# Sums of the up projections' weights: from VectorE to accumulating DMA transfers in DRAM

## The reference, cut to what matters

```python
h = x @ w_in + b_in                       # x: 1024 x 1024, w_in: 1024 x 5376
q_a, k_a, v_a, gate_a, q_b, k_b, v_b, gate_b, mg_a, mg_b = split(h)
o_a = swa_sink_attention(rope(q_a), rope(k_a), v_a, sinks) * silu(gate_a)   # 1024 x 512
y_a = o_a @ w_up_a                        # 512 -> 1024
o_b = stick_breaking_attention(q_b, k_b, v_b) * silu(gate_b)                # 1024 x 512
y_b = o_b @ w_up_b                        # 512 -> 1024
merged = sigmoid(mg_a) * y_a + sigmoid(mg_b) * y_b
out = layer_norm(alpha * x + merged @ w_out)
```

## Time and profile before

| what | value |
|---|---|
| median of 3 runs | 721.74 us (721.46 to 722.67) |
| the profiled execution | 722.17 us, span 720.4 us |
| PE busy | 707.2 us (98%) |
| DVE, ACT, POOL busy | 561.4, 446.7, 103.7 us |
| DMA moved | 77.27 MB, mean 107 GB/s |

### The profile page before, as it was taken

How to read it: one execution, slowest core, us unless ns; L and a number is a source line. 1 busy time by engine, 2 the same in 40 slices (tenths; PEclk the granted TensorE clock), 3 DMA queues, 4 the chain that set the end, 5 groups by cost and what they waited for, 6 DMA issues and landing times.

```text
span 720.4 us, 10882 instructions
## 1 busy us (share of the span) xinstructions
PE 707.2 (98%) x3998; PEld 577.8 (80%) x3998; DVE 561.4 (78%) x782; ACT 446.7 (62%) x776; POOL 103.7 (14%) x130
## 2 busy tenths in 40 slices
PE   8999999999999999999999999999998999999996
PEld 6888877777888888788888888888887888888885
DVE  6999788765987987898889784557779999990644
ACT  6954477776867767777686764565577655750421
POOL 0000000000322232132222310000000000000882
PEclk9999999999999999999999999999999999999999
DMA  8235332231100101020113214666324555830451
GB/s 297 113 90 126 107 94 84 74 98 43 50 31 30 60 30 59 3 88 16 45 30 117 74 45 144 219 233 208 117 82 153 170 166 159 310 118 1 160 190 58
DMA packets 44916, 77.27 MB, mean 107 GB/s; under 512 B 12352, under 2 KB 16960, under 8 KB 44864
## 3 DMA queue, kind: packets, MB, share of 16 engines
q1 hardware_dynamic: 44864, 76.59, 33.0%
HBM read 55.60 MB, written 18.87 MB: 103 GB/s over the span
## 4 chain that ended last, share of the span: by engine, by line
PE 96%; DVE 2%; DMA 1%; issue 1%; ACT 0%; SPq 0%; POOL 0%; POOLq 0%; DVEq 0%; ACTq 0%
PE ps L209 26%; PE ps L211 26%; PE ps L210 26%; PE ps L1789 5%; PE ps L1801 5%; PE ps L1774 4%; PE ps L1718 1%; PE ps L1730 1%; PE ps L1699 1%; DMA xr<-in_xt 1%; DVE keep L1455 1%; PE ps L1753 0%; PE ps L1687 0%; DVE o_t L1594 0%; DVE o_t L1585 0%
## 5 line engine op out<-in xcount | busy, mean ns | idle before, releaser
L209 PE MATMUL ps<-x_hi,w_hi 128*128 128x512 f32 x416 | 167.2, 402 | 1.9 <-DVE x_lo L1362 1.9
L211 PE MATMUL ps<-x_hi,w_lo 128*128 128x512 f32 x416 | 162.5, 391 | 0.0
L210 PE MATMUL ps<-x_lo,w_hi 128*128 128x512 f32 x416 | 162.2, 390 | 0.0
L1254 DVE TENSOR_TENSOR w_lo<-raw,w_hi 128x512 fp32r<-128x512 f32 x144 | 97.8, 694 | 47.9 <-ACT w_hi L772 47.4
L209 PE MATMUL ps<-t_ops,w_hi 128*128 128x512 f32 x288 | 115.8, 402 | 2.3 <-issue 2.3
L211 PE MATMUL ps<-t_ops,w_lo 128*128 128x512 f32 x288 | 113.2, 393 | 0.0
L210 PE MATMUL ps<-t_ops,w_hi 128*128 128x512 f32 x288 | 112.9, 392 | 0.0
L1455 DVE TENSOR_TENSOR_SCAN keep<-keep 128x895 f32<-128x895 f32 (+4 forms) x64 | 85.9, 1373 | 15.4 <-POOL keep L729 15.4
L209 PEld LDWEIGHTS ps<-x_hi,w_hi 128*128 128x128 f32 x416 | 78.2, 188 | 17.9 <-issue 3.4
L211 PEld LDWEIGHTS ps<-x_hi,w_lo 128*128 128x128 f32 x416 | 78.1, 188 | 16.8
L210 PEld LDWEIGHTS ps<-x_lo,w_hi 128*128 128x128 f32 x416 | 78.3, 188 | 14.6
(11 more groups left out here) (196 smaller groups left out, 1182.2 us busy)
## 6 DMA issues: line engine op xcount, KB each, us to landing
raw<-in_w SPq DMA_DIRECT2D x50, 256.0 KB, 2.9
raw<-in_w SPq DMA_DIRECT2D x24, 512.0 KB, 3.8
sig_m<-sig_d SPq DMA_DIRECT2D x16, 512.0 KB, 4.7
sig_d<-sig_m SPq DMA_DIRECT2D x28, 256.0 KB, 2.7
xr<-in_xt SPq DMA_DIRECT2D x16, 256.0 KB, 6.1
o_t<-o_d SPq DMA_DIRECT2D x8, 512.0 KB, 4.9
raw<-in_xn SPq DMA_DIRECT2D x8, 512.0 KB, 3.7
out<-o_t SPq DMA_DIRECT2D x16, 256.0 KB, 2.2
```

Source lines behind the costliest of these rows:

```text
L209: pe.matmul(out, w_hi, x_hi, start=first, stop=False, skip_group_check=goes_on)
L210: pe.matmul(out, w_hi, x_lo, start=False, stop=False, skip_group_check=goes_on)
L211: return pe.matmul(out, w_lo, x_hi, start=False, stop=last, skip_group_check=goes_on)
L1254: dve.tensor_tensor(ring_slot(w_lo, q), part_of(q), ring_slot(w_hi, q).bitcast(F32), ALU.subtract).then_inc(part_lo, 1)
```

## The change

For each of the four up pairs the seven weight operands are seven loads of 256 KB from DRAM, in the order of the products; DVE makes no weight sums for them. Three of the seven are quarters as they are. Four come from DRAM buffers (`up_sum_d`, 1 MB each, all four pairs in one) that POOL fills after the input has been split: three copies, then two accumulating transfers that wait for them, then a copy, an accumulating transfer and another one, each waiting for the one before. Two sums keep another sign than before; it is made good by the sign of two operands of the other side, by a scale of -1 when two products are read out, and by one subtraction. Five buffers take the loads in turn. The high parts of the weights go one to each product from product 138 on.

```diff
 def next_parts(q):
-    return {0: (q + 3, q + 4), 5: (), 6: (q + 3,)}.get(q % NP, (q + 4,)) if q < ALL_PRODUCTS - 4 else ()
+    if q >= LAST_PAIR + 5:
+        return (q + 4,) if q < ALL_PRODUCTS - 4 else ()
+    return {0: (q + 3, q + 4), 5: (), 6: (q + 3,)}.get(q % NP, (q + 4,))
+UP_RAWS = 5
+def up_raw_loads(q):
+    if q < LAST_PAIR + 3:
+        return {LAST_PAIR: (N_PRODUCTS, N_PRODUCTS + 1), LAST_PAIR + 1: (N_PRODUCTS + 2, N_PRODUCTS + 3),
+                LAST_PAIR + 2: (N_PRODUCTS + 4,)}.get(q, ())
+    return (q + 4 + UP_RAWS,) if q + 4 + UP_RAWS < ALL_PRODUCTS else ()
...
+        def up_raw(q):
+            n = (q - N_PRODUCTS) % UP_RAWS
+            return (raw[:, 1, half(0)], raw[:, 0, half(0)], w_x[:], raw[:, 0, half(1)], raw[:, 1, half(1)])[n]
+        up_tiles = w[UP_0:UP_0 + KT].rearrange("(j m) p c -> m p j c", m=2)
+        def up_quarter(m, kh):
+            return up_tiles[m][:, :, half(kh)]
...
+            def load_up(q):
+                n = q - N_PRODUCTS
+                if n < UP_RAWS:
+                    sp.wait_ge(part_lo, LAST_PAIR + (4, 5, 3, 6, 7)[n])
+                else:
+                    sp.wait_ge(part_lo, q - UP_RAWS + 1)
+                if n == 2:
+                    sp.wait_ge(w_sum, 4 * N_PAIRS)
+                    sp.wait_ge(up_summed, 16 * 8)
+                j, which = n // NP, ORDER[n % NP]
+                if which in up_sum_d:
+                    src = up_sum_d[which][:, j, :]
+                else:
+                    src = w[UP_0 + 2 * j + (which == 4)][:, half(which != 1)]
+                sp.dma_start(up_raw(q), src).then_inc(up_in[n % UP_RAWS], 16)
...
-                if pos < 2 and i + 1 < ALL_PAIRS:
+                if pos < 2 and i + 1 < N_PAIRS:
                     load_a1(i + 1, pos)
-                if pos == 2 and i + 1 < ALL_PAIRS:
+                if pos == 2 and i + 1 < N_PAIRS:
                     load_a2(i + 1)
+                for n in up_raw_loads(q):
+                    load_up(n)
...
+            pool.wait_ge(x_lo_done, 2 * KT)
+            pool.dma_start(up_sum_d[5], up_quarter(1, 0)).then_inc(up_summed, 16)
+            pool.dma_start(up_sum_d[7], up_quarter(0, 0)).then_inc(up_summed, 16)
+            pool.dma_start(up_sum_d[3], up_quarter(0, 1)).then_inc(up_summed, 16)
+            pool.wait_ge(up_summed, 16 * 3)
+            pool.dma_start(up_sum_d[5], up_quarter(1, 1), accum_op=ALU.add).then_inc(up_summed, 16)
+            pool.dma_start(up_sum_d[7], up_quarter(1, 0), accum_op=ALU.add).then_inc(up_summed, 16)
+            pool.wait_ge(up_summed, 16 * 5)
+            pool.dma_start(up_sum_d[6], up_sum_d[5]).then_inc(up_summed, 16)
+            pool.wait_ge(up_summed, 16 * 6)
+            pool.dma_start(up_sum_d[6], up_quarter(0, 0), accum_op=ALU.add).then_inc(up_summed, 16)
+            pool.wait_ge(up_summed, 16 * 7)
+            pool.dma_start(up_sum_d[3], up_sum_d[6], accum_op=ALU.add, max_dma_last_dim=4 * HALF).then_inc(up_summed, 16)
             for s in range(STEPS):
                 cut_causal(s)
...
                     act.activation(up_other(pos) if pos % 2 else up_made(b), ps[:, 2 * (q % 2):2 * (q % 2) + 2, :],
-                                   ACT.Copy).then_inc(bank_read, 1)
+                                   ACT.Copy, scale=-1.0 if pos in (4, 6) else 1.0).then_inc(bank_read, 1)
...
-                    dve.tensor_tensor(o, o, up_sum(2, ab), ALU.subtract).then_inc(u_raw[t], 1)
+                    dve.scalar_tensor_tensor(out=o, in0=up_sum(2, ab), scalar=-1.0, in1=o, op0=ALU.mult,
+                                             op1=ALU.subtract).then_inc(u_raw[t], 1)
...
-                if pos in (4, 5) and i + 1 < ALL_PAIRS:
+                if pos in (4, 5) and i + 1 < N_PAIRS:
                     weight_sums(i + 1, pos == 4)
```

More of the change, by code:

```diff
@@ L315, in build @@
         sig_d = nc.dram_tensor("sig_d", (KT, 2, P, SEQ), F32, kind="Internal").ap()
+        up_sum_d = {n: nc.dram_tensor(f"up_sum{n}_d", (P, UP_PAIRS, HALF), F32, kind="Internal").ap()
+                    for n in (5, 6, 7, 3)}
         gate_d = nc.dram_tensor("gate_d", (GROUP, P, SEQ), F32, kind="Internal").ap()
@@ L418, in ring_slot @@
             return t[:, q // 2 % 2, half(q % 2)]
+        def up_raw(q):
[4 more added lines that the diff above has]
+            return up_tiles[m][:, :, half(kh)]
         def part_of(q):
+            if q >= N_PRODUCTS:
+                return up_raw(q)
             which = ORDER[q % NP]
@@ L456, in build, with up_arrived @@
         a11_in, a12_in, a2_in = sem("a11_in"), sem("a12_in"), sem("a2_in")
+        up_in = (a2_in, a11_in, raw_in[0], a12_in, raw_in[1])
+        up_summed = sem("up_summed")
         const_in = sem("const_in")
+        def up_arrived(n):
+            return up_in[n % UP_RAWS], 16 * (n // UP_RAWS + 1 + (1 if n % UP_RAWS in (2, 4) else N_PAIRS))
         first_in = [[sem(f"first_in{n}_{i}") for i in range(2)] for n in range(2)]
@@ L759, in part_high @@
                 i, which = q // NP, ORDER[q % NP]
-                if which == 1:
+                if i >= N_PAIRS:
+                    act.wait_ge(*up_arrived(q - N_PRODUCTS))
+                elif which == 1:
                     act.wait_ge(a11_in, 16 * (i + 1))
@@ L1230, in add_block @@
                     o = up_made((0, 2, 1)[k])
-                    dve.tensor_tensor(o, o, up_other(2 * k + 1), ALU.add).then_inc(block_sum, 1)
+                    dve.tensor_tensor(o, o, up_other(2 * k + 1),
+                                      ALU.subtract if k == 1 else ALU.add).then_inc(block_sum, 1)
                     return
@@ L1283, in up_sums @@
                             dve.wait_ge(o_back[k], 16)
-                    dve.tensor_tensor(o, quarter_of(0, 1), quarter_of(0, 0), ALU.subtract).then_inc(u_raw[t], 1)
+                    dve.tensor_tensor(o, quarter_of(0, 0), quarter_of(0, 1), ALU.subtract).then_inc(u_raw[t], 1)
                 elif t == 2:
@@ L1287, in up_sums @@
                     dve.wait_ge(z_done, STEPS)
-                    dve.tensor_tensor(o, quarter_of(1, 1), up_sum(1, ab), ALU.subtract).then_inc(u_raw[t], 1)
+                    dve.scalar_tensor_tensor(out=o, in0=up_sum(1, ab), scalar=-1.0, in1=quarter_of(1, 1), op0=ALU.mult,
+                                             op1=ALU.subtract).then_inc(u_raw[t], 1)
                 elif t == 3:
```

## The result

The changed kernel took 729.64 us, median of six runs from 725.25 to 730.88; the kernel before took 722.12 beside it. The ratio is 1.0097, with a 95% interval from 1.0081 to 1.0113: the change costs 1%, about 7.5 us, where 2.3 us less was forecast. The runs of this kernel lie 5.6 us apart, those of the kernel before 1.2; the profiled execution is the shortest of the six, so its trace shows 3.1 us of the loss. The five longer runs have no trace; what they lost beyond that is taken up with the experiments.

A forecast was written before the change was run, and what follows sets the result against it. PE's own work bounds the kernel (96% of the last chain's span), with 3.72 us lost at product 142. Profiled 722.17 less 2.29 gives 719.9; the median, 0.43 lower, gives 719.5 us, range 718.2 to 723.2.

The forecast's parts named there:

- I take no wait of PE from that: SP's early loads beside POOL's transfers: the tightest, a21 and a22 of pair 1, lands after 6.2 us, 7.7 allowed; cost zero.
- The share: The a21 and a22 load beside POOL's transfers gets half of the transfer engines, its data taking 4.2 us instead of 2.1.
- the turns that the prediction left open: Sharing between SP's and POOL's queues: even interleaving keeps the forecast; sums' packets taking three times as long cause a loss.
- fourth rival: Pair 1's load lands after 10.4 us; PE waits 2.7 near 52 us, slow clock adds 1.65: 723.8 us; chance 0.13.
- second rival: Early contention costs PE 1 to 2 us without a clock step: 720.5 to 721.5 us; chance 0.16.
- The transition: At up products 142 and 143, two shorter PE waits at full clock let product 143 start 2.29 us earlier.
- first rival: The clock falls at the two shorter waits near products 142 and 143, leaving 0.64 us gain: 721.1 us; chance 0.10.
- the third: The change does nothing: the wait at product 142 is on something that stays: 721.7 us; chance 0.05.
- the fourteen other sums: DVE's weight sums standing from 557.50 us on, where PE waits for nothing: removing them is worth nothing.
- The changed instruction in the other side's sums: On DVE ahead of the block sum, the form with a scalar takes longer: 0.10 us taken for two.
- The order of ACT's high parts: In ACT's queue behind the read of product 140, one high part remains instead of two, saving 0.52 us.
- fifth rival: POOL's transfers outlast 179.94 us and hold the attention's first mask: some 750 us at five times the load's rate; chance 0.04.

The follow-up runs named there:

- the chain alone: The kernel before with POOL's eight transfers added near the start, their sums unread: 729.7 us, ratio 1.0118.
- without the chain: The changed kernel without POOL's eight transfers, up loads taking weight quarters in place of sums: 719.7 us against 721.74, ratio 0.9974.
- second profile: The changed kernel run once more, unchanged, on a chip that ran no other experiment: 725.78 us against 721.56, ratio 1.006.
- the old order of the high parts: The changed kernel without POOL's eight transfers and with the up weights' high parts ordered as in the kernel before: 720.11 us against 721.64, ratio 0.9976.
- the first five transfers: The kernel before with only three copies and two accumulating transfers of POOL's eight: 723.55 us, ratio 1.0025.
- the three copies: The kernel before with only the first three of POOL's transfers, plain copies of 1 MB: 721.73 us against 721.64, ratio 0.9998.

## Why the prediction was wrong

**The step that failed** is the one on SP's transfers beside the chain, "I take no wait of PE from that", a term of zero. It measured 5.43 us in the profiled execution. By the medians it was 8.0 for the chain alone (729.7 against 721.74, one chip), and for the changed kernel about 10 in its first session and 6 in its second, against the 719.7 without the chain. Three things in it were off.

- The tightest load was not that of a21 and a22. That one took 8.6 us, and its 7.7 us of room had by then grown by the wait at 48.11, so PE didn't wait for it. The a11 of pair 1, issued 4 us earlier, has 2.5 us of room, because ACT's queue has the PSUM read close behind its high part. I looked at DVE's users of loads only.
- The share was off. With the prediction's 2.0 us of fixed time, an estimate, the data of the a21 load took 8.6 - 2.0 = 6.6 us in place of 2.1, a third of the engines and not a half; that of a11 took 4.8 in place of 0.9, about a fifth. The row that I leaned on, 402 GB/s from one queue, showed that capacity is shared; nothing showed how. The DMA view from 36 to 42 us bears on the turns that the prediction left open: 517 packets of the chain took 99.7% of 16 engines, 0.19 us each, and 144 packets of loads in the kernel before 13.8%, 0.09 us each. One packet of each in turn would leave a load a third, by estimate; that fits the a21 load and not the smaller share of a11, so how the queues take turns stays open.
- It wasn't one wait. The fourth rival had the kind of mechanism right, a late load of pair 1, with another load and one wait of 2.7 us for it. The first wait delays the swaps on SP, the swaps land late and hold DVE's low parts and SP's next loads, and so on for three more while the chain lasts. The rival's landing of 10.4 us and its clock step did not occur in the first profiled execution, where the granted clock stayed at 1.00 from 40 to 90 us and from 545 to 565. In the second profile its clock step did, behind a wait of 2.67 us; that this is close to the rival's 2.7 is luck, for the wait is at 71 us and a later one of the chain of delays. The second rival, 1 to 2 us of contention, was short of the 5 to 10 that it cost.

The Trainium skill, DMA: Bandwidth & Descriptors, section "Issuing engines are not separate DMA queues", spoke against the hiding, and the trace agrees: POOL's transfers came out of SP's share (the a21 load took 8.6 us in place of 4.1). What this case adds is that, by the estimate above, the queues did not share evenly.

**What was right.** The transition: 2.29 forecast, 2.37 in the traces. The first wait was to be 0.83 and is 0.74; from product 142 to 143 it was to be 3.32 us and is 560.56 - 557.23 = 3.33, at full clock. The first rival did not happen, nor the third: ACT's wait for DVE's block sum fell from 2.72 us to 1.39, 1.33 where 1.24 was forecast, and the wait of PE fell from 2.07 to 0.73 without the chain and to 0.74 with the old order of the high parts too. ACT in order of time, changed kernel:

```profile
553.18 0.64 ACT L971 ACTIVATE sig_m<-sig_m 128x512 f32<-128x512 f32 x1 [1.39 <-DVE sig_m L1306]
```

One reading beside it was off, at no cost: two of the fourteen other sums stand at 548.96 and 549.56, not behind 557.50, but behind the block sum. The changed instruction in the other side's sums was put at 0.10 for two and cost nothing. DVE in order of time has the same sum as a plain subtraction in the kernel before, and in its new form in the changed one:

```profile
538.41 1.22 DVE L1295 TENSOR_TENSOR o_t<-o_t,raw_c 128x1024 f32<-128x1024 f32 x1
...
543.84 1.22 DVE L1368 SCALAR_TENSOR_TENSOR o_t<-raw_c,o_t 128x1024 f32<-128x1024 f32 x1
```

Both took 1.22 us. The order of ACT's high parts was put at 0.52 and shows 0.54. The sixteen more loads on SP cost nothing: the end is 162.9 us behind product 143 in both traces. The chain was to end at 60 to 100 us and ended at 79, and the mask did not wait for it, so the fifth rival fell.

With the early term taken from another run, the 8.0 us that the chain alone cost, the sum is 721.74 - 2.3 + 8.0 = 727.4 us; the two sessions of the changed kernel came out on either side, at 725.78 and 729.64.

## What to carry to other kernels

A background transfer is hidden only when every load and swap beside it has room for the delay; here loads took up to 2.4 times as long. List the users of all the loads in the stretch, on each engine's queue, take the one with the least room, and follow its delay through the queues to the next loads. When that room is small, look first for a stretch where no load with little room is under way: the same eight transfers, begun 86 or 177 us later, cost nothing that could be measured. Here an accumulating transfer in DRAM took about twice the engine time of a copy; count its packets before you price one.

## What the hardware showed that I had not expected

- Two accumulating transfers from DRAM to DRAM filled the engines (share 1.01) at 179 GB/s, copies in the same place at 353 (share 0.94). The two took 1056 packets, 528 for each MB, where a copy of 1 MB took 272 (page, part 3: 1872 packets with the first five transfers, 816 with the three copies).
- Beside two accumulating transfers a load of 256 KB took 6.8 us in place of 2.8, one of 512 KB 8.6 in place of 4.1. The latter's data had, by estimate, a third of the engines, though it was one queue against one.
- The loss from the same instructions was 7.5 us in one session and 4.2 in another, and single runs of the changed kernel went from 724.36 to 730.88. Why, the runs don't settle; the one trace of the second session shows a fall of the granted clock as a part of it.
- A PE wait of 2.33 us left the granted clock at 1.00 in one run, and one of 1.8 us in another was followed by 0.50, so the length of the wait alone did not tell.
